# A streaming encoder step: half of w_out loaded per tile, and its SBUF given to gather slots and to a copy of the rows that the dots read

## The chip, the cores and the metric

The kernel runs on one core of one Trainium2 chip. The metric is the device time of one execution in microseconds (us). The engines are called by the profile's names: PE (TensorE), PEld (its weight loads), DVE (VectorE), ACT (ScalarE), POOL (GpSimd) and SP (SyncE).

## The reference

One layer over a prompt of 1024 rows and a sample of 32 rows, all in float32, D = 1024. The mixer (mLSTM and sliding-window attention, then w_out of 1024x1024) is followed by PEER, a mixture of 16384 single-row experts:

```
x = x + concat(mLSTM heads, attention heads) @ w_out
h = rmsnorm(x)
q = (h @ w_q)                         # 8 heads, 256 wide
idx = the 16 best of 128 x 128 experts for each row and head
a = gelu(sum over d of peer_u[idx] * h)       # 16 dots of 1024 for each row and head
x = x + sum over heads and k of (softmax weight * a) * peer_v[idx]
y = rmsnorm(x)
```

So each of the 1056 rows reads 8 x 16 rows of peer_u and as many of peer_v, 4 KB each.

## The kernel before, in words

**Tiles and groups.** Work is done in 9 tiles: 8 of 128 prompt rows and the sample's 32 (tile 8, SAMPLE). For PEER a tile is cut into blocks of 32 rows (SUB). 32 rows x 4 heads fill the 128 partitions, so a block has two groups of 4 heads, and there are 66 groups. In a group, k runs over the 16 chosen experts. For every (group, k) POOL issues one gather of peer_u (L582) and one of peer_v (L593): an indirect DMA of 128 rows of 4 KB, 512 KB, whose row numbers it reads from the SBUF tile `idx`. POOL alternates: U of group g + 1, then V of group g.

**Slots.** The tile `ring` holds NU = 6 U slots and NV = 7 V slots of 4 KB a partition. POOL waits on `u_free` before it writes into a U slot that is still used, and on `v_free` for a V slot, in one program order.

**DVE, ACT, PE for each slot t = 16 g + k.** DVE multiplies the U slot by `h2p` and sums up into `dots` (L1261, "the dot"; the accumulator is read by an instruction of its own). `h2p` is a PSUM tile that holds the block's 32 rows four times, once for each head. PE writes it in `spread_rows` (L1603) with 16 instructions, once every two groups, from the tile `ch`. Between dots DVE does a piece of `topk` for group g + 3 (11 of 16 slots), and at a group's turn `weigh` (L1210 to L1216), which makes the weights `wk` out of gelu (ACT, L821) and softmax. PE multiplies the V slot by `wk` into `acc` (L1657). In the same order of slots all engines do steps of the next tile's mixer, query projection and scores. The tables PE_AT, ACT_AT and DVE_AT and the function slot_of say at which slot. `attn_out` (L1504, L1505) is the last product of attention, `cat_transpose` and `h2_transpose` are L1513, `out_proj` is L1531, `residual` L1131, the query product L1549.

**Where h2p turns.** `spread_rows(q)` is called at k = 15 of an even group, and PE waits there for `dots_done`, since the dots still read `h2p`. DVE waits for `h2p_set` ahead of the next group's first dot. When g is odd DVE does `weigh(g)` and the first stage of `topk(g + 3)` before that wait ("ahead").

**Weights and SP.** One SBUF tile, `weights`, holds w_in in the start phase, then w_out (32 KB a partition, `wout_s`) and w_q (64 KB). w_out is loaded once, and used by tiles 1 to 8; tile 0 has its own copy in the ring. SP issues all plain DMAs in program order. In tile m these are `load_p(m)` (projection rows from a DRAM scratch), `store_y(m - 2)` and `load_x(m)`. Between tiles 3 and 4 `project_again` projects the rows of tiles 4 to 8 anew ("reprojection", L1365), with w_in streamed in pieces.

Of the kernel before, what the change touches and what calls it, by code (L numbers as in the profile page):

```python
# [48 lines left out]
SUB = 32  # L49
NU = 6  # L50
NV = 7
GROUPS = 2 * (SEQ // SUB + 1)
# [123 lines left out]
def program(nc, x_prompt, x_sample, cache_k, cache_v, st_c, st_n, st_m, norm_mix_w, w_in, if_bias, mnorm_w, sinks,  # L176
# [15 lines left out]
    with ExitStack() as ctx:  # L192
# [3 lines left out]
        def sem(name):  # L196
            return ctx.enter_context(nc.semaphore(name))
# [3 lines left out]
        win_s = [weights[:, DC * c0:DC * (c0 + w)].rearrange("p (k c) -> p k c", k=DC) for c0, w in PC]  # L201
        wout_s = weights[:, 0:DC * D].rearrange("p (k c) -> p k c", k=DC)
        wq_s = weights[:, DC * D:].rearrange("p (k c) -> p k c", k=DC)
        ring = sb("ring", [P, NU + NV, D])
        pj = sb("pj", [P, PJ])
# [12 lines left out]
        t8 = reg[:, 0:1024].rearrange("p (k t) -> p k t", k=DC)  # L218
        qrow = reg[:, 1024:1536]
        pT = pj[:, 0:2048].rearrange("p (h b t) -> p h b t", h=QH, b=2)  # L220
        qT = pj[:, 0:2048].rearrange("p (c t) -> p c t", c=QC)
# [69 lines left out]
        po = [sc[:, 4 * b:4 * b + 4, :].rearrange("p c k -> p (c k)") for b in range(4)]  # L291
        po += [part[:, :]] + [ring[:, NU + 4, 0:512]] + [a[:, h * 512:h * 512 + 512] for a in (ring[:, NU + 5, :], ring[:, NU + 6, :]) for h in range(2)]
        first = [pj[:, 0:512], pj[:, 512:1024], vx[:, :, 0:MD], pj[:, 1024:1536], pj[:, 1536:2048], pj[:, 2048:PJ]]
# [20 lines left out]
        proj_out = [sem(f"proj_out{b}") for b in range(10)]  # L314
        wout_in, wq_in = sem("wout_in"), sem("wq_in")
        keysT_ready, keysT_copied = sem("keysT_ready"), sem("keysT_copied")
        state_in, stateT_ready, state_set = sem("state_in"), sem("stateT_ready"), sem("state_set")
# [15 lines left out]
        wpiece_in, po_again_out = [sem(f"wpiece_in{i}") for i in range(3)], [sem("po_again_out0"), sem("po_again_out1")]  # L333
        topk_done, h2p_set = sem("topk_done"), sem("h2p_set")
        u_in = [sem(f"u_in{i}") for i in range(NU)]
# [22 lines left out]
        def _(sp):  # L358
# [79 lines left out]
            def load_wout():  # L438
                sp.dma_start(wout_s, w_out[0].rearrange("(k p) c -> p k c", p=P)).then_inc(wout_in, 16)

            def project_again():

                load_x1_again(FIRST)
                sp.wait_ge(query_ready, 4 * FIRST)
# [78 lines left out]
            for b in range(10):  # L523
                sp.wait_ge(proj_out[b], stored(b, len(UNITS)))
            for m in range(2, TILES):
                if m == FIRST:
# [13 lines left out]
                if m != FIRST:  # L540
                    load_p(m)
                store_y(m - 2)
                load_x(m)
# [12 lines left out]
        def _(pool):  # L556
# [16 lines left out]
            def gather_u(g, k):  # L573

                n = TOPK * g + k
                if k == 0:
                    pool.wait_ge(topk_done, g + 1)
                if n >= NU:
                    pool.wait_ge(u_free, n - NU + 1)
                elif n >= NU - 2:  # L580
                    pool.wait_ge(query_ready, 3)
                pool.indirect_dma_start(ring[:, n % NU, :], None, u_d,  # L582
                                        bass.IndirectOffsetOnAxis(ap=idx[:, g % 4, k:k + 1], axis=0)).then_inc(u_in[n % NU], 16)

            def gather_v(g, k):

                n = TOPK * g + k
                if n >= NV:
                    pool.wait_ge(v_free, n - NV + 1)
                elif n >= NV - 3:  # L590
                    for b in {NV - 3: (5,), NV - 2: (6, 7), NV - 1: (8, 9)}[n]:
                        pool.wait_ge(proj_out[b], stored(b, len(UNITS)))
                pool.indirect_dma_start(ring[:, NU + n % NV, :], None, v_d,  # L593
                                        bass.IndirectOffsetOnAxis(ap=idx[:, g % 4, k:k + 1], axis=0)).then_inc(v_in[n % NV], 16)
# [11 lines left out]
        def _(act):  # L606
# [211 lines left out]
            def gelu(g):  # L818
# [3 lines left out]
                act.drain().then_inc(gelu_ready, 1)  # L822

            def gather_parts(q):

                s = q % 4
                other = slice((s + 2) % 4 * SUB, (s + 2) % 4 * SUB + SUB)
                act.wait_ge(v_free, 2 * TOPK * (q + 1))
                if q == 0:
                    for b in (4,):  # L830
                        act.wait_ge(proj_out[b], stored(b, len(UNITS)))
                S.copy(part[other, :], acc[other, 512:])
                act.drain().then_inc(part_ready, 1)
# [21 lines left out]
            for s, i, r in ACT_AT:  # L855
                if r >= EARLY_END:
                    mix(s, i, 0)
                    if s == "query_copy" and i == 1:
                        keep_first()
            keep_scores(0)  # L860

            steps = by_slot(ACT_AT)
            for g in range(-1, GROUPS):
                for k in range(TOPK):
# [9 lines left out]
                    if k == TOPK - 1 and g + 1 < GROUPS:  # L874
                        gelu(g + 1)
                    for s, i, m in steps.get(t, ()):
                        mix(s, i, m)
# [25 lines left out]
        def _(dve):  # L903
# [347 lines left out]
            for g in range(-1, GROUPS - 1):  # L1251
                for k in range(TOPK):
# [5 lines left out]
                    if k == 0 and g % 2:  # L1258
                        dve.wait_ge(h2p_set, (g + 1) // 2 + 1)
                    dve.wait_ge(u_in[n % NU], 16 * (n // NU + 1))  # L1260
                    V.scalar_tensor_tensor(ring[:, n % NU, :], ring[:, n % NU, :], 1.0, h2p[:, :], ALU.mult, ALU.mult,  # L1261
                                           accum_out=dots[:, (g + 1) % 2, k:k + 1]).then_inc(u_free, 1)
# [35 lines left out]
        def _(pe):  # L1298
# [120 lines left out]
            def mix(s, i, m):  # L1419
# [100 lines left out]
                elif s == "out_proj":  # L1520
                    half, k0 = i // 4, i % 4 * 2
                    if i == 0:
# [4 lines left out]
                    if m == 0 and i % 4 == 0:  # L1527
                        pe.wait_ge(wout_first_in[half], 16)
                    for k in (k0, k0 + 1):
                        w = wout_first[half][:, k, :] if m == 0 else wout_s[:, k, half * 512:half * 512 + 512]  # L1530
                        last = T.matmul(mx[0:n, 2 + half, :], t8[:, k, 0:n], w, start=k == 0, stop=k == DC - 1)  # L1531
# [61 lines left out]
            def spread_rows(q):  # L1593
# [3 lines left out]
                if q > 0:  # L1597
                    pe.wait_ge(dots_done, 2 * q)
                pe.wait_ge(h2_ready, m + 1)
# [39 lines left out]
            for g in range(-1, GROUPS):  # L1639
                for k in range(TOPK):  # L1640
# [3 lines left out]
                    if k == 2 and g > 0 and g % 2 == 0:  # L1644
                        gather_parts(g // 2 - 1)
                    if k == TOPK - 1 and g % 2 == 0 and g + 2 < GROUPS:
                        spread_rows(g // 2 + 1)
                    if g >= 0 and t > 0:
# [4 lines left out]
                        for n in (0, 1) if t == 1 else (t,):  # L1653
                            pe.wait_ge(v_in[n % NV], 16 * (n // NV + 1))
                            for half in range(2):
                                cols, j = slice(half * 512, half * 512 + 512), (g // 2 + 2 * half) % 4 * SUB
                                last = T.matmul(acc[j:j + SUB, cols], wk[:, g % 2, n % TOPK, :], ring[:, NU + n % NV, cols],  # L1657
                                                start=g % 2 == 0 and n % TOPK == 0, stop=g % 2 == 1 and k == TOPK - 1)
# [59 lines left out]
```

## Time and profile before

| | |
|---|---|
| timed runs, median of 3 | 3127.24 us (3126.11 to 3127.49) |
| span of the profiled execution | 3386.3 us |
| mean granted clock of PE | 0.811 |
| gathers (L582 and L593) | 2112, 1107.43 MB |
| all DMA traffic | 1197.02 MB, 353 GB/s over the span |

The profiled execution is one of its own. The profile gives its span alone, from the first to the last instruction, and no time around it: 3386.3 us, 259 us more than the median of the timed runs. Durations of instructions come from the profiled one.

### The profile page before, as it was taken

The page shows a single profiled execution, that of the slowest core. Times are in us where ns is not written, and L with a number is a line of the kernel's source. Part 1 is how long each engine was busy: PE and PEld are TensorE (multiplying, and loading weights), DVE is VectorE, ACT ScalarE, POOL GpSimd, SP SyncE. Part 2 cuts the span into 40 slices and gives each one's busy share as a digit, 9 for nine tenths or more (in the row PEclk, how much of TensorE's full clock was granted, in tenths as well). Part 3 has the DMA queues.
Part 4 walks back from the last instruction along what each step waited for, and adds up shares of the span by engine and source line. Part 5 has one row for each costly group of instructions (what it writes and reads, how often), then busy time and mean ns, then how long its engine had stood idle before and what let it go on. Part 6 is the DMA issues. An engine that isn't in the chain of part 4 may idle for free.

```text
span 3386.3 us, 33673 instructions
## 1 busy us (share of the span) xinstructions
PE 2600.2 (77%) x10989; PEld 1007.2 (30%) x10989; DVE 2120.6 (63%) x5282; ACT 556.3 (16%) x1093; POOL 1995.2 (59%) x2128
## 2 busy tenths in 40 slices
PE   8996886678678899987876876678676776686666
PEld 4562351225222533223432331124212331121101
DVE  1256657766676666657667757676667666676653
ACT  2211111211121131122012111111111011111001
POOL 0026556666666566665656666666666666666665
PEclk9997897789677899997987887788667886677667
DMA  6479999999999999999999999999999999999998
GB/s 230 146 275 371 336 338 374 362 371 343 378 351 365 342 400 407 409 382 353 362 329 346 380 354 381 367 364 345 384 360 360 370 365 376 358 368 370 371 363 332
DMA packets 348919, 1197.02 MB, mean 353 GB/s; under 512 B 37760, under 2 KB 54408, under 8 KB 346952
## 3 DMA queue, kind: packets, MB, share of 16 engines
q0 software_dynamic: 304128, 1107.43, 86.7%
q1 hardware_dynamic: 44616, 87.45, 7.0%
q8 instruction: 86, 1.41, 0.2%
q14 instruction: 89, 0.73, 0.1%
HBM read 1180.69 MB, written 14.15 MB: 353 GB/s over the span
## 4 chain that ended last, share of the span: by engine, by line
PE 33%; DVE 16%; issue 13%; POOL 12%; DMA 9%; another core or an unknown queue 8%; DVEq 6%; ACT 1%; ACTq 0%; SPq 0%; POOLq 0%
PE acc L1657 11%; PE mx L1549 7%; DVE ring L1261 7%; POOL ring L593 6%; POOL ring L582 6%; DMA ring<-in_peer_v_dram,idx 5%; DVEq L1148 4%; DMA ring<-in_peer_u_dram,idx 4%; PE mx L1365 3%; PE mx L1531 2%; PE acc L1341 2%; PE mx L1560 2%; PE acc L1328 1%; PE h2p L1603 1%
## 5 line engine op out<-in xcount | busy, mean ns | idle before, releaser
L1657 PE MATMUL acc<-ring,wk 128*32 128x512 f32 x4224 | 1362.6, 742 | 525.6 <-DMA ring<-in_peer_v_dram,idx 289.4
L1261 DVE SCALAR_TENSOR_TENSOR ring<-ring,h2p 128x1024 f32<-128x1024 f32 x1056 | 1273.8, 1215 | 565.4 <-DMA ring<-in_peer_u_dram,idx 315.8
L593 POOL DMA_INDIRECT ring<-in_peer_v_dram,idx x1056 | 997.1, 944 | 707.7 <-issue 269.7
L582 POOL DMA_INDIRECT ring<-in_peer_u_dram,idx x1056 | 996.3, 943 | 667.1 <-issue 292.9
L1657 PEld LDWEIGHTS acc<-ring,wk 128*32 128x32 f32 x4224 | 217.8, 122 | 1406.6 <-issue 670.8
L1549 PE MATMUL mx<-reg,weights 128*128 128x128 f32 x1792 | 256.7, 297 | 40.9 <-issue 38.6
L1549 PEld LDWEIGHTS mx<-reg,weights 128*128 128x128 f32 x1792 | 230.8, 206 | 145.7 <-issue 145.7
L1531 PE MATMUL mx<-weights,reg 128*128 128x512 f32 (+1 forms) x256 | 133.0, 643 | 3.5 <-issue 3.5
L1365 PE MATMUL mx<-weights 128*128 128x512 f32 (+1 forms) x288 | 126.9, 585 | 0.0
L821 ACT ACTIVATE gl<-dots 128x16 f32<-128x16 f32 x66 | 14.2, 216 | 637.5 <-issue 346.1
L1603 PE MATMUL h2p<-ch,ident 32*32 32x512 f32 x528 | 86.7, 708 | 36.6 <-issue 18.9
L1560 PE MATMUL mx<-kT,pj 128*32 128x128 f32 x1040 | 69.4, 313 | 32.9 <-issue 25.3
L781 ACT COPY pj<-mx 128x512 f32<-128x512 f32 x32 | 18.7, 585 | 432.0 <-remote 182.7
L1261 DVE DVE_READ_ACCUMULATOR ring<-ring,h2p 128x1 f32 x1056 | 86.9, 82 | 0.0
L821 ACT ACT_TABLE_LOAD x66 | 84.7, 1283 | 6.5 <-issue 1.1
L815 ACT ACT_TABLE_LOAD x61 | 78.3, 1283 | 19.1 <-issue 11.3
L1365 PEld LDWEIGHTS mx<-weights 128*128 128x128 f32 x288 | 53.4, 195 | 75.8 <-issue 74.3
L1531 PEld LDWEIGHTS mx<-weights,reg 128*128 128x128 f32 (+1 forms) x256 | 44.1, 189 | 96.4 <-issue 96.4
L1560 PEld LDWEIGHTS mx<-kT,pj 128*32 128x32 f32 x1040 | 50.1, 123 | 64.6 <-issue 54.8
L1224 DVE TENSOR_TENSOR xt<-xt,acc 32x1024 f32<-32x1024 f32 x33 | 40.1, 1216 | 45.0 <-PE acc L1612 32.2
L1087 DVE TENSOR_REDUCE s<-mx 128x4 f32<-128x1024 f32 (+1 forms) x18 | 21.0, 1174 | 58.9 <-remote 46.6
L1365 PE MATMUL mx<-weights,reg 128*128 128x512 f32 (+1 forms) x96 | 47.4, 642 | 12.4 <-DMA weights<-in_w_in_dram 6.6
(310 smaller groups left out, 2400.3 us busy)
## 6 DMA issues: line engine op xcount, KB each, us to landing
ring<-in_peer_u_dram,idx POOLq DMA_INDIRECT x1056
ring<-in_peer_v_dram,idx POOLq DMA_INDIRECT x1056
weights<-in_peer_w_q_dram SPq DMA_DIRECT2D x7, 2048.0 KB
weights<-in_w_in_dram SPq DMA_DIRECT2D x5, 2048.0 KB, 18.2
weights<-in_w_in_dram SPq DMA_DIRECT2D x10, 1024.0 KB
ring<-in_peer_w_q_dram SPq DMA_DIRECT2D x8, 1024.0 KB, 5.6
xt<-in_x_prompt_dram SPq DMA_DIRECT2D x8, 512.0 KB
ring<-in_w_out_dram SPq DMA_DIRECT2D x2, 2048.0 KB, 14.2
```

Source lines behind the costliest of these rows:

```text
L582: pool.indirect_dma_start(ring[:, n % NU, :], None, u_d, bass.IndirectOffsetOnAxis(ap=idx[:, g % 4, k:k + 1], axis=0)).then_inc(u_in[n % N ...
L593: pool.indirect_dma_start(ring[:, NU + n % NV, :], None, v_d, bass.IndirectOffsetOnAxis(ap=idx[:, g % 4, k:k + 1], axis=0)).then_inc(v_in[ ...
L815: S.activation(ew[:, :], top[:, g % 3, :], ACT.Exp, bias=ntop[:, g % 3:g % 3 + 1], accum_out=ez[:, 0:1])
L821: S.activation(gl[:, :], dots[:, g % 2, :], ACT.Gelu)
L1148: dve.drain()
L1261: V.scalar_tensor_tensor(ring[:, n % NU, :], ring[:, n % NU, :], 1.0, h2p[:, :], ALU.mult, ALU.mult, accum_out=dots[:, (g + 1) % 2, k:k + ...
L1365: last = T.matmul(bank, hT1_again[i][:, 4 * half + k, :], wpiece[(2 * p + half) % 3][:, k, 0:w], start=half + k == 0, stop=half == 1 and k ...
L1531: last = T.matmul(mx[0:n, 2 + half, :], t8[:, k, 0:n], w, start=k == 0, stop=k == DC - 1)
L1549: last = T.matmul(mx[:, i // 4, i % 4 * P:i % 4 * P + n], w, t8[:, k, 0:n], start=k == 0, stop=k == DC - 1)
L1560: last = T.matmul(mx[q:q + SUB, i, col:col + NK], qT[:, c, i * SUB:(i + 1) * SUB], kT[:, c % 2, :], start=True, stop=True)
L1603: last = T.matmul(h2p[j * SUB:(j + 1) * SUB, cols], ident[r, r], ch[m % 2][r, cols], start=True, stop=True)
L1657: last = T.matmul(acc[j:j + SUB, cols], wk[:, g % 2, n % TOPK, :], ring[:, NU + n % NV, cols], start=g % 2 == 0 and n % TOPK == 0, stop=g ...
```

## The change

Of w_out only the first 4 of 8 row blocks (WK = 4) stay in `weights`. The other four, 512 KB each, are loaded again in each tile 1 to 8 by `pass_wout(m)` on SP: three into parts of `pj` and `reg` once attention is through (`attn_ready`), the last into `ch[m % 2]` once its transposes are done (`rows_transposed`). `out_proj` takes the products of both halves with blocks 0 to 6 first and with block 7 last. The 16 KB a partition that come free hold a seventh U slot, an eighth and a ninth V slot and `h2s`, an SBUF copy of `h2p` which ACT makes in `keep_rows`. The dot reads `h2s` in place of `h2p`. PE fills `h2p` at k = 4 of the even group, waiting only for the copy before; ACT copies it behind the gelu of the last group that reads the old rows. `project_again` gets a wait for `mixed_ready`.

```diff
-NU = 6
-NV = 7
+RU, RV = 6, 7
+NU = 7
+NV = 9
+WK = 4
...
-        wout_s = weights[:, 0:DC * D].rearrange("p (k c) -> p k c", k=DC)
+        wout_s = weights[:, 0:WK * D].rearrange("p (k c) -> p k c", k=WK)
...
+        spare = [weights[:, (WK + i) * D:(WK + i + 1) * D] for i in range(NU - RU + NV - RV)]
+        h2s = weights[:, (WK + 3) * D:(WK + 4) * D]
+        u_slot = [ring[:, b, :] for b in range(RU)] + spare[:NU - RU]
+        v_slot = [ring[:, RU + b, :] for b in range(RV)] + spare[NU - RU:]
...
+        wout_pass = [pj[:, 0:D], pj[:, D:2 * D], reg[:, D:2 * D]]
...
+            def pass_wout(m):
+                sp.wait_ge(attn_ready, m + 1)
+                for j in range(3):
+                    k = WK + j
+                    sp.dma_start(wout_pass[j], w_out[0, k * P:(k + 1) * P, :]).then_inc(wout_pass_in, 16)
+                sp.wait_ge(rows_transposed, 2 * m + 1)
+                sp.dma_start(ch[m % 2][:, :], w_out[0, (DC - 1) * P:DC * P, :]).then_inc(wout_last_in, 16)
...
             def project_again():
+                sp.wait_ge(mixed_ready, FIRST)
                 load_x1_again(FIRST)
...
             for m in range(2, TILES):
...
+                pass_wout(m)
                 store_y(m - 2)
                 load_x(m)
...
+            def keep_rows(q):
+                act.wait_ge(h2p_set, q + 1)
+                if q > 0:
+                    act.wait_ge(dots_done, 2 * q)
+                S.copy(h2s, h2p[:, :])
+                act.drain().then_inc(h2s_ready, 1)
...
                     if k == TOPK - 1 and g + 1 < GROUPS:
                         gelu(g + 1)
+                        if g >= 0 and g % 2 == 0 and g + 2 < GROUPS:
+                            keep_rows(g // 2 + 1)
...
-                        dve.wait_ge(h2p_set, (g + 1) // 2 + 1)
+                        dve.wait_ge(h2s_ready, (g + 1) // 2 + 1)
                     dve.wait_ge(u_in[n % NU], 16 * (n // NU + 1))
-                    V.scalar_tensor_tensor(ring[:, n % NU, :], ring[:, n % NU, :], 1.0, h2p[:, :], ALU.mult, ALU.mult,
+                    V.scalar_tensor_tensor(u_slot[n % NU], u_slot[n % NU], 1.0, h2s, ALU.mult, ALU.mult,
...
-                    half, k0 = i // 4, i % 4 * 2
+                    pairs = [(i // 4, i % 4 * 2 + a) for a in range(2)]
+                    if m > 0:
+                        pairs = [divmod(2 * i + a, DC - 1) for a in range(2)] if i < DC - 1 else [(0, DC - 1), (1, DC - 1)]
...
+                    if m > 0 and i == WK // 2:
+                        pe.wait_ge(wout_pass_in, 16 * 3 * m)
+                    if m > 0 and i == DC - 1:
+                        pe.wait_ge(wout_last_in, 16 * m)
...
                 if q > 0:
-                    pe.wait_ge(dots_done, 2 * q)
+                    pe.wait_ge(h2s_ready, q)
...
-                    if k == TOPK - 1 and g % 2 == 0 and g + 2 < GROUPS:
+                    if k == 4 and g >= 0 and g % 2 == 0 and g + 2 < GROUPS:
                         spread_rows(g // 2 + 1)
```

## Rows read from the trace of the kernel before

**Rows 1.** The page's first part: busy time, share of the span, instructions.
```profile
PE 2600.2 (77%) x10989; PEld 1007.2 (30%) x10989; DVE 2120.6 (63%) x5282; ACT 556.3 (16%) x1093; POOL 1995.2 (59%) x2128
```

**Rows 2.** The page's costliest groups: busy, mean ns, idle before and its releaser.
```profile
L1657 PE MATMUL acc<-ring,wk 128*32 128x512 f32 x4224 | 1362.6, 742 | 525.6 <-DMA ring<-in_peer_v_dram,idx 289.4
L1261 DVE SCALAR_TENSOR_TENSOR ring<-ring,h2p 128x1024 f32<-128x1024 f32 x1056 | 1273.8, 1215 | 565.4 <-DMA ring<-in_peer_u_dram,idx 315.8
L593 POOL DMA_INDIRECT ring<-in_peer_v_dram,idx x1056 | 997.1, 944 | 707.7 <-issue 269.7
L582 POOL DMA_INDIRECT ring<-in_peer_u_dram,idx x1056 | 996.3, 943 | 667.1 <-issue 292.9
```

**Rows 3.** The list of waits: us in total, times, longest.
```profile
POOL ring L582 <- DVEq L1204: 198.1, 6, 189.3
...
DVE ring L1261 <- remote: 89.0, 14, 9.7
...
DVE ring L1261 <- PE h2p L1603: 63.4, 14, 15.2
```

**Rows 4.** Timeline of POOL in the start: two long waits.
```profile
209.67 0.94 POOL L582 DMA_INDIRECT ring<-in_peer_u_dram,idx  x1 [9.13 <-DVE ring L1261]
...
259.67 0.94 POOL L593 DMA_INDIRECT ring<-in_peer_v_dram,idx  x1 [19.19 <-DMA proj_scratch<-ring]
```

**Rows 5.** Timeline of POOL, then of DVE, in a quiet stretch.
```profile
3163.36 0.94 POOL L582 DMA_INDIRECT ring<-in_peer_u_dram,idx  x1 [0.31 <-issue]
3164.61 0.94 POOL L593 DMA_INDIRECT ring<-in_peer_v_dram,idx  x1 [0.30 <-issue]
3165.85 0.94 POOL L582 DMA_INDIRECT ring<-in_peer_u_dram,idx  x1 [0.31 <-issue]
...
3164.78 1.22 DVE L1261 SCALAR_TENSOR_TENSOR ring<-ring,h2p 128x1024 f32<-128x1024 f32 x1 [1.32 <-DMA ring<-in_peer_u_dram,idx]
...
3167.35 1.22 DVE L1261 SCALAR_TENSOR_TENSOR ring<-ring,h2p 128x1024 f32<-128x1024 f32 x1 [1.34 <-DMA ring<-in_peer_u_dram,idx]
```

**Rows 6.** Windows: busy of PE, PEld, DVE, ACT, POOL; clock, DMA share, GB/s.
```profile
1300.00:1350.00 50.00, 47.10 (x154) 15.57 (x153) 31.75 (x75) 9.45 (x15) 32.54 (x35) 0.98 1.03 409
2400.00:2450.00 50.00, 33.91 (x105) 7.36 (x106) 30.83 (x76) 8.70 (x11) 33.55 (x36) 0.64 1.02 399
```

**Rows 7.** Timeline: gathers, and DVE instructions that began within half a microsecond.
```profile
259.23 1.22 DVE L1261 SCALAR_TENSOR_TENSOR ring<-ring,h2p 128x1024 f32<-128x1024 f32 x1 [3.29 <-DMA ring<-in_peer_u_dram,idx]
...
289.35 0.43 DVE L1193 TENSOR_TENSOR cand<-cand,i2f 128x256 f32<-128x256 f32 x1
289.44 1.15 POOL L593 DMA_INDIRECT ring<-in_peer_v_dram,idx  x1 [0.31 <-issue]
...
1018.36 0.69 DVE L1216 TENSOR_TENSOR wk<-rept,coef 128x512 f32<-128x512 f32 x1
1018.49 1.38 POOL L593 DMA_INDIRECT ring<-in_peer_v_dram,idx  x1 [0.30 <-PE acc L1657]
...
2477.14 0.93 POOL L582 DMA_INDIRECT ring<-in_peer_u_dram,idx  x1 [0.31 <-DVE ring L1261]
2477.28 0.69 DVE L1216 TENSOR_TENSOR wk<-rept,coef 128x512 f32<-128x512 f32 x1
```

**Rows 8.** Groups by form: busy, mean ns, idle before.
```profile
L1216 DVE TENSOR_TENSOR wk<-rept,coef 128x512 f32<-128x512 f32 x66 | 45.7, 693 | 6.3 <-issue 0.8 <-remote 0.5
...
L1035 DVE SCALAR_TENSOR_TENSOR pj<-pj,reg 128x512 f32<-128x512 f32 x8 | 5.5, 685 | 0.7 <-ACTq L721 0.7
...
L781 ACT COPY pj<-mx 128x512 f32<-128x512 f32 x32 | 18.7, 585 | 432.0 <-remote 182.7 <-PE mx L1549 171.2 <-issue 78.1
```

**Rows 9.** DMA issues with time to landing; timeline of PE in tile 4.
```profile
weights<-in_w_in_dram SPq DMA_DIRECT2D x1, 1056.0 KB, 17.3
...
1593.54 0.39 PE L1504 MATMUL mx<-vprev,pj 128*128 128x64 f32 x2
...
1614.44 1.12 PE L1531 MATMUL mx<-weights,reg 128*128 128x512 f32 x2
```

## What I predict, and how the numbers come about

> **What bounds the kernel now.** I read the busy line first: no engine is full, PE is busiest with 77% and it idles in between; POOL has 59%, DVE 63% [rows 1]. Shares say little here, because the same four workers take turns on every pair of gathers (one row set of peer_u for a dot on DVE, one of peer_v for a product on PE). So I read the groups of the page for POOL. Its 2112 gathers are busy 997.1 + 996.3 = 1993 us and have 707.7 + 667.1 = 1375 us of idle time in front of them [rows 2]. The timeline of a quiet stretch shows that two gathers issued without any wait start 1.245 us apart, 0.94 busy and 0.30 to 0.31 between [rows 5]. So 2111 x 0.31 = 654 us of that idle time is the cost of issuing, 189 us is the wait for the first indices [rows 3], and 1375 - 654 - 189 = about 532 us is waiting for a free slot. Two of these waits, 28 us together, belong to the start: a V slot that the projection still used, and the first U slots [rows 4]. That leaves about 504 us. POOL's chain is thus 190 + 1993 + 654 + 532 = 3369 us, and with the tail it is the span of 3386: **the kernel is set by POOL's issue, at 2.49 us a pair, plus 504 us of waiting for slots.**
>
> The second bound lies just under it. In the same stretch, where DVE waits for nothing but data, the dots start every 2.55 to 2.57 us while POOL issues every 2.49 [rows 5]: transfers land at 1.05 MB / 2.56 = 410 GB/s, the rate that the windows with the DMA engines at 1.03 also show (409) [rows 6]. A window of quieter work has 399 GB/s at 1.02. So POOL cannot win more than it loses to the DMA engines, 0.06 us a pair or about 65 us in all.
>
> **The change, part by part.**
>
> *Three more slots (U 6 to 7, V 7 to 9).* They act on the 504 us alone. A V slot stays taken while PE does the tile's own work, a U slot while DVE stands at the turn of a row block. Two V slots are 5 us of issue more before POOL stops, one U slot 2.5 us. In the reprojection (the window from 1300 to 1350 stands for it: PE busy 47.1 of 50 us and DMA at 1.03) they can do nothing, since PE and DMA are full [rows 6]; I leave 50 us of waits there and 50 us for stalls longer than the slots. Of 504 some 400 go, less the 65 that DMA does not allow: **gain 335 us**, bounds 150 (slots fill again wherever PE is behind) and 440.
>
> *Spread in PSUM at index 4, copy h2s.* Before, spread_rows waits for the last dot and DVE for spread_rows: 63.4 + 89.0 = 152 us in 28 waits of DVE [rows 3]. Now the spread is done 11 slots earlier, and behind the last dot stands gelu and then an ACT copy of 128x1024. The copy of 128x512 takes 585 ns from PSUM [rows 8], so twice that, 1.2 us. DVE meanwhile has weigh (its product alone is 693 ns [rows 8]) and stage 0 of topk, so the copy costs nothing there; without that cover it would be 33 x 1.2 = 40 us. ACT has 16% of busy time [rows 1], 39 us more hide. The 152 us are waits of DVE, and they reach POOL only as U slots that come free late: they are within the 504 and I don't count them again. What is late next is gelu and the product's coefficients, unchanged.
>
> *The dot reads two SBUF tensors.* This is the disputed cost, in two halves. The duration: a two-SBUF SCALAR_TENSOR_TENSOR of 128x512 takes 685 ns, no more than those with a PSUM input, so I keep 1.215 us [rows 8, 2]. The other half is POOL. The trace has 2112 gathers, nearly all of 0.94 us, and the longer ones have a two-SBUF DVE instruction over their start. A gather that began 0.13 us after a 0.69 us product of rept and coef took 1.38; one that began 0.09 us after a 0.43 us product of cand and i2f took 1.15; one that began 0.14 us before such a product took 0.93 [rows 7]. In each, the gather runs on about 0.12 us before the DVE instruction's end: the stretch is (DVE duration - 0.12 - distance of the starts). Today's dot, whose second input is in PSUM, stretches none: a gather that began 0.44 us after a dot took 0.94 [rows 4, 7], and the mean of all is 943 to 944 ns [rows 2]. For a dot of 1.215 us the stretch is up to 1.04 and 0.52 on average. If gathers start at random against dots, 1056 x 1.04 / 3180 = 35% of them are caught: 0.18 us each, **380 us in all**. That is the upper bound. The lower is near 0.06 us a pair, 65 us: where dots come every 2.56 us and POOL could issue every 2.49, POOL's starts drift forward against the dots by 0.07 us a pair and meet a dot at its trailing end, where a stretch costs just the drift, and then stay there [rows 5]. Topk and the mixing steps break that rhythm often. I take the middle, **200 us**.
>
> The Trainium skill, page "SBUF — State Buffer", section "Who interferes with whom", says that a DVE instruction with at most one SBUF input doesn't contend with GpSimd, and that one with two contends with a GpSimd instruction that reads SBUF. By that rule, the trace agrees for gathers that start under such an instruction (1.38 and 1.15 against 0.94) and speaks against this edit; the sum above would be the same.
>
> *w_out in parts.* Four row blocks of 512 KB for each of 8 tiles, less 2 MB of the one load: 14.7 MB, 36 us at 410 GB/s. POOL, slowed by the stretches, leaves the DMA engines room, so most of it hides; without that room it is 36. They stand in SP's queue behind attn_ready and ahead of store_y and load_x. A load of 1056 KB landed 17.3 us after issue, 61 GB/s [rows 9], so three parts take 20 to 25 us. In tile 4 PE's attention ends at 1593.9 and the third step of out_proj, now the first to need them (the first two use the four resident rows), starts at 1614.4 [rows 9]: up to 5 us late, and load_x behind them can hold DVE's residual, with the dots queued behind it. Other tiles have 25 us or more. I take **40 us** for traffic and lateness together, bounds 0 and 100. project_again now waits for mixed_ready of tile 3, and behind it on SP only the wait for query_ready, which comes later anyway: nothing. The order of out_proj's 16 products changes, not their number: nothing.
>
> **Sum.** -335 + 200 + 40 = -95 us on the profiled 3386 (-2.8%). The timed median is 3127, 259 us less for the same work. Either issue and transfers are quicker without the profiler (then the terms stand), or there are fewer waits to take away (then 504 - 259 = 245 are left, the gain is about 180, and the sum +60). Between them, leaning to the first: -57 us, **3070 us**.
>
> **Rivals.**
> - *The stretch costs little and the slots give all they can* (gathers lock to the dots' ends). -335 + 65 + 20 = -250, 3127 - 190 = 2940 after the same discount. For it: the steady rhythm. Against: 11 of 16 dots have topk pieces between them.
> - *The stretch at random, and too few waits to pay for it.* POOL then needs 2.49 + 0.36 = 2.85 us a pair. With a gain of 220, between my 335 and the lower bound, 380 + 40 - 220 = +200; where PE or DMA is the bound anyway (a third, by the 504 us and the windows like the reprojection) stretches hide: +125, about 3250. It decides as soon as the mean stretch of a gather passes (gain - 40) / 2112: 0.14 us in the profile's budget, 0.07 to 0.10 if the timed run has half of the waits.
> - *DMA is the bound of the timed run already*: slots bring nothing, the stretch hides, and 14.7 MB are added: 3127 + 5 to 40, say 3145.
> - *The dot slows down.* Here is no row of a two-SBUF product with an accumulator. At twice 1.215 us DVE is busy 2120.6 + 1273.8 = 3394 us [rows 1, 2] and becomes the bound: about 3450. For it nothing but that gap in the rows; the 685 ns row speaks against. The Trainium skill, "Vector Engine (DVE) Microarchitecture Reference", section "Points that are easy to get wrong", says that this instruction with two sources in SBUF that aren't bf16 runs at half throughput. By that rule, the trace disagrees where there is no accumulator; with one no run here shows it.
>
> **How the numbers follow.** Forecast 0.37, locked gathers 0.20, random stretch 0.27, DMA-bound 0.10, slow dot 0.06. A difference under 0.2% can't be told from none here. The forecast and the locked case are faster (0.57, of which 0.02 falls within 0.2%); DMA-bound gives 0.05 to no change; the rest is slower: 0.55, 0.07, 0.38. The range takes the forecast with its bounds and reaches toward both neighbours: 2960 to 3260.
>
> **What would show it.** L593 and L582: mean above 943 ns (1.04 at 200 us of stretch, 1.13 at 380), with their idle time down from 1375 to about 950. L1261: still 1215 ns, and its waits for PE's spread gone. The row of keep_rows near 1.1 us x33. Out_proj's first product with a streamed row: a wait in tile 4 at most. The forecast is wrong if the idle time of the gathers does not fall, if the stretch is at its upper bound, or if L1261 changes its duration.

## The result, and the profile after

The changed kernel takes 3251.66 us (median of 4 runs, 3249.96 to 3255.37); the kernel before took 3126.68 us beside it (4 runs, 3124.94 to 3127.49). The ratio is 1.0401 (1.0387 to 1.0416): 125 us slower, where 3070 us and a gain of 57 us were forecast. The measured time lies at the far end of the stated range (2960 to 3260), and it is the time that the second rival gave.

The page of the changed kernel, its busy line, traffic, the chain that ended last, the groups that answer to [rows 1, 2], and two issue lines (count, kilobytes each where given, us to landing):

```profile
PE 2571.2 (79%) x10989; PEld 958.5 (30%) x10989; DVE 2142.5 (66%) x5282; ACT 589.5 (18%) x1126; POOL 2304.2 (71%) x2128
...
DMA packets 353017, 1211.72 MB, mean 373 GB/s; under 512 B 38272, under 2 KB 54920, under 8 KB 351048
...
POOL 33%; PE 30%; DMA 19%; issue 12%; DVE 4%; DVEq 1%; ACT 1%; SPq 0%; ACTq 0%; POOLq 0%
...
L1294 DVE SCALAR_TENSOR_TENSOR ring<-ring,weights 128x1024 f32<-128x1024 f32 x906 | 1106.0, 1223 | 578.5 <-DMA ring<-in_peer_u_dram,idx 549.3
...
L604 POOL DMA_INDIRECT ring<-in_peer_u_dram,idx x906 | 977.3, 1079 | 523.7 <-issue 263.5
L615 POOL DMA_INDIRECT ring<-in_peer_v_dram,idx x822 | 902.5, 1098 | 270.6 <-issue 216.2
...
L615 POOL DMA_INDIRECT weights<-in_peer_v_dram,idx x234 | 259.9, 1111 | 71.9 <-issue 62.2
...
L604 POOL DMA_INDIRECT weights<-in_peer_u_dram,idx x150 | 162.7, 1084 | 60.4 <-issue 43.3
...
L1576 PE MATMUL mx<-weights,reg 128*128 128x512 f32 (+1 forms) x128 | 71.3, 673 | 0.1
...
ring<-in_peer_u_dram,idx POOLq DMA_INDIRECT x906, 7.5
...
pj<-in_w_out_dram SPq DMA_DIRECT2D x16, 512.0 KB, 8.1
```

L604, L615 and L1294 are the U gather, the V gather and the dot; an operand in the memory that w_out gave up is named `weights`. POOL's 2112 gathers are now busy 2302 us (mean 1.09) where they had 1993, and idle for 523.7 + 60.4 + 270.6 + 71.9 = 927 us where they had 1375 [rows 2]. With 654 us of issue gaps and 190 before the first indices, 83 us of slot waits are left. POOL's chain is 190 + 2302 + 654 + 83 = 3229, and with a tail of 19 it is the span of 3248.2. The execution behind this span took 3249.96 us: **span and time of one execution lie 2 us apart, not 259.** The 259 us of the profile ahead of the prediction must be a difference between executions.

The timeline of POOL and of DVE in a quiet stretch of the changed kernel answers to [rows 5, 7]:

```profile
3061.30 1.82 POOL L615 DMA_INDIRECT ring<-in_peer_v_dram,idx  x1 [0.30 <-PE acc L1702]
3063.43 0.93 POOL L604 DMA_INDIRECT ring<-in_peer_u_dram,idx  x1 [0.30 <-issue]
3064.66 0.99 POOL L615 DMA_INDIRECT ring<-in_peer_v_dram,idx  x1 [0.30 <-PE acc L1702]
3065.96 1.05 POOL L604 DMA_INDIRECT ring<-in_peer_u_dram,idx  x1 [0.30 <-issue]
...
3061.08 1.23 DVE L1294 SCALAR_TENSOR_TENSOR ring<-ring,weights 128x1024 f32<-128x1024 f32 x1 [1.61 <-DMA ring<-in_peer_u_dram,idx]
3062.23 0.08 DVE L1294 DVE_READ_ACCUMULATOR ring<-ring,weights 128x1 f32 x1
...
3063.62 1.22 DVE L1294 SCALAR_TENSOR_TENSOR weights<-weights 128x1024 f32<-128x1024 f32 x1 [0.72 <-DMA weights<-in_peer_u_dram,idx]
...
3065.78 0.42 DVE L1226 TENSOR_TENSOR cand<-cand,i2f 128x256 f32<-128x256 f32 x1
```

The first gather begins 0.22 us after a dot and takes 1.82 us: the rule of the prediction gives 1.23 - 0.12 - 0.22 = 0.89 over 0.94. The third begins 1.04 us after a dot and takes 0.99, by the rule 0.94 + 0.06. The fourth meets no dot but a product of two SBUF tiles that the kernel before has too: 0.42 - 0.12 - 0.18 over 0.94 is 1.06, and it takes 1.05. The dot itself is no longer for it (1.22 to 1.23 us). POOL waits 0.30 us before each, which is the bare issue gap, so every stretch moves all that follows.

Counted over the whole trace of the changed kernel, 680 gathers begin between 0.07 and 1.05 us after a dot's start, and 679 of them last within 0.05 us of what the rule gives (with 0.943 for a gather without a stretch). The 824 gathers that begin up to 1.1 us after a dot's start carry 291 us of stretch. In before_2, a trace of the kernel before from a chip of the same speed, the 814 such gathers carry none.

### The profile page after: what moved, and what is told of

The parts are those of the page before. It is cut to its first block, busy times and chain, and to the rows that moved or that the text cites. A ratio compares the mean times of both kernels' runs of the same rounds, so it can differ in the third digit from the quotient of the medians.

```text
span 3248.2 us, 33803 instructions
## 1 busy us (share of the span) xinstructions
PE 2571.2 (79%) x10989; PEld 958.5 (30%) x10989; DVE 2142.5 (66%) x5282; ACT 589.5 (18%) x1126; POOL 2304.2 (71%) x2128
## 4 chain that ended last, share of the span: by engine, by line
POOL 33%; PE 30%; DMA 19%; issue 12%; DVE 4%; DVEq 1%; ACT 1%; SPq 0%; ACTq 0%; POOLq 0%
POOL ring L604 14%; POOL ring L615 14%; PE acc L1702 10%; DMA ring<-in_peer_v_dram,idx 10%; PE mx L1594 6%; DMA ring<-in_peer_u_dram,idx 4%; POOL weights L615 3%; DMA weights<-in_peer_v_dram,idx 3%; POOL weights L604 2%; PE mx L1576 2%; PE acc L1374 2%; PE mx L1398 1%; PE acc L1361 1%; PE h2p L1648 1%; DVE ring L1294 1%
## 5 line engine op out<-in xcount | busy, mean ns | idle before, releaser
L1294 DVE SCALAR_TENSOR_TENSOR ring<-ring,weights 128x1024 f32<-128x1024 f32 x906 | 1106.0, 1223 | 578.5 <-DMA ring<-in_peer_u_dram,idx 549.3
L1702 PE MATMUL acc<-ring,wk 128*32 128x512 f32 x3288 | 1088.4, 757 | 499.2 <-DMA ring<-in_peer_v_dram,idx 423.4
L604 POOL DMA_INDIRECT ring<-in_peer_u_dram,idx x906 | 977.3, 1079 | 523.7 <-issue 263.5
L615 POOL DMA_INDIRECT ring<-in_peer_v_dram,idx x822 | 902.5, 1098 | 270.6 <-issue 216.2
L1702 PEld LDWEIGHTS acc<-ring,wk 128*32 128x32 f32 x3288 | 151.4, 121 | 1221.2 <-DMA ring<-in_peer_v_dram,idx 876.1
L1702 PE MATMUL acc<-weights,wk 128*32 128x512 f32 x936 | 311.1, 757 | 122.9 <-DMA weights<-in_peer_v_dram,idx 107.5
L615 POOL DMA_INDIRECT weights<-in_peer_v_dram,idx x234 | 259.9, 1111 | 71.9 <-issue 62.2
L1294 DVE SCALAR_TENSOR_TENSOR weights<-weights 128x1024 f32<-128x1024 f32 x150 | 183.6, 1224 | 92.5 <-DMA weights<-in_peer_u_dram,idx 90.0
L604 POOL DMA_INDIRECT weights<-in_peer_u_dram,idx x150 | 162.7, 1084 | 60.4 <-issue 43.3
L1294 DVE DVE_READ_ACCUMULATOR ring<-ring,weights 128x1 f32 x906 | 74.6, 82 | 0.0
L1576 PE MATMUL mx<-weights,reg 128*128 128x512 f32 (+1 forms) x128 | 71.3, 673 | 0.1
L1257 DVE TENSOR_TENSOR xt<-xt,acc 32x1024 f32<-32x1024 f32 x33 | 40.1, 1216 | 24.0 <-PE acc L1657 23.2
```

The source lines that it names most:

```text
L604: pool.indirect_dma_start(u_slot[n % NU], None, u_d, bass.IndirectOffsetOnAxis(ap=idx[:, g % 4, k:k + 1], axis=0)).then_inc(u_in[n % NU], 16)
L615: pool.indirect_dma_start(v_slot[n % NV], None, v_d, bass.IndirectOffsetOnAxis(ap=idx[:, g % 4, k:k + 1], axis=0)).then_inc(v_in[n % NV], 16)
L1257: V.tensor_tensor(xt[m % 2][r, :], xt[m % 2][r, :], acc[r, :], ALU.add)
L1294: V.scalar_tensor_tensor(u_slot[n % NU], u_slot[n % NU], 1.0, h2s, ALU.mult, ALU.mult, accum_out=dots[:, (g + 1) % 2, k:k + 1]).then_inc(u ...
```

## The experiments

The theory: the dot's second SBUF input stretches the gathers and makes POOL the bound, and the slots bring little, because the timed runs lack the waits that they were to remove. Rivals: the cost comes from the streamed w_out, from the early spread with its copy, or from the longer queue of gathers. The dot's operand and the streamed w_out were run alone, the slots on top of the streamed w_out, whose memory they need; the early spread was never run without the copy. The runs fell on four chips (A to D here). On A and B the kernel before takes 3125.6 (9 runs) and 3126.9 us (9), as in the comparison; on C and D it takes 3414.7 (21) and 3393.7 us (8). The recorded texts call C and D slow chips. Each chip was used in one session only, so what belongs to the chip and what to the session isn't told apart. A ratio is always against the kernel before on the same chip.

All results first; slot waits are worked out from each page as above (idle time of the gathers - 654 - 190). Gathers and slot waits are in us.

| run | chip | ratio to before (interval) | span profiled | gathers busy | slot waits |
|---|---|---|---|---|---|
| before_2 | A | one run, 3128.7 us | 3127.0 | 1996 | 268 |
| wout_only_2 | B | 1.0117 (1.0101 to 1.0132) | 3163.9 | 1995 | 306 |
| slots_only_2 | A | 1.0099 (1.0084 to 1.0115) | 3156.8 | 1999 | 293 |
| fewer_slots | A | 1.0206 (1.0192 to 1.0220) | 3181.0 | 1998 | 322 |
| dot_sbuf_2 | A | 1.0441 (1.0417 to 1.0465) | 3270.5 | 2328 | 79 |
| copy_only_2 | B | 1.0473 (1.0452 to 1.0495) | 3274.7 | 2327 | 85 |
| before_again | C | one run, 3421.8 us | 3420.1 | 1993 | 565 |
| wout_only | C | 0.9997 (0.9977 to 1.0017) | 3409.8 | 1995 | 553 |
| slots_only | C | 1.0110 (1.0087 to 1.0134) | 3454.4 | 1995 | 598 |
| dot_sbuf | C | 1.0044 (1.0026 to 1.0062) | 3425.5 | 2350 | 214 |
| after_again | D | 1.0091 (1.0063 to 1.0120) | 3421.8 | 2326 | 232 |
| copy_only | D | 1.0034 (1.0014 to 1.0054) | 3394.9 | 2336 | 197 |

**The dot with two SBUF inputs alone** (dot_sbuf on C, dot_sbuf_2 on A). The kernel before, whose dot reads other SBUF data in place of `h2p`: a row of a constant mask, 128 wide and read 8 times. It leaves out the right dots, so the output is not the reference's; sizes, waits and traffic are the same.

```diff
-V.scalar_tensor_tensor(ring[:, n % NU, :], ring[:, n % NU, :], 1.0, h2p[:, :], ALU.mult, ...
+V.scalar_tensor_tensor(ring[:, n % NU, :], ring[:, n % NU, :], 1.0, triu[:, :].unsqueeze(1).broadcast_to([P, DC, P]), ALU.mult, ...
```

> The kernel before with one edit: the dot's second input is an SBUF constant (triu, repeated 8 times) in place of h2p in PSUM. It leaves the right dots out, so y is not the reference's; indices, gathers, waits and all durations' shapes are those of before. Theory (a dot with two SBUF inputs holds up the start of a gather): POOL's busy time rises by 280 to 380 us, of which the 270 us of slot waits hide a part: 3230 to 3330 us. Rival (the loss of the changed kernel comes from w_out's traffic and its place in SP's queue): 3127. Rival (the dot itself is slower with two SBUF inputs): L1261's mean above 1.3 us; the theory says 1.22.

> The kernel before with the dot's second input an SBUF constant; it leaves the right dots out. Theory A: on a slow chip +0.4% again, since a POOL that issues later leaves PE its instructions (issue idle 195 in place of 300) and the 360 us of stretch fit into 570 us of waits; on a chip that takes 3127 there are 270 us of waits, so +120 to +200 us: 3250 to 3330. Theory B (the loss of the changed kernel has another cause than the dot's operand): +0.4% there too.

On A this one edit costs 4.4%, 143 us, more than the whole change: inside the 120 to 200 us of the theory, and against the rivals. The groups of its page:

```profile
L1261 DVE SCALAR_TENSOR_TENSOR ring<-ring,triu 128x1024 f32<-128x1024 f32 x1056 | 1287.8, 1223 | 719.9 <-DMA ring<-in_peer_u_dram,idx 671.5
...
L582 POOL DMA_INDIRECT ring<-in_peer_u_dram,idx x1056 | 1148.1, 1087 | 565.9 <-issue 310.6
L593 POOL DMA_INDIRECT ring<-in_peer_v_dram,idx x1056 | 1180.3, 1118 | 357.0 <-issue 261.2
```

Its gathers are 332 us longer than before_2's, and its slot waits fell by 189 us with not one slot more: 332 - 189 = 143. POOL comes late, so the slots are free when it comes. On C the same stretch (357 us longer) is met by 351 us fewer waits, and the edit costs 0.4%: dot_sbuf's 3230 to 3330 us, expected before C was known to be slower, were missed.

**The kernel before, again** (before_again on C, before_2 on A).

> The kernel before, unchanged, for a trace beside its timed runs. The profiled execution on which the prediction rested had a span of 3386 us, its timed runs 3127. In the changed kernel span and time are 2 us apart (3248.2 and 3249.96). Expected: span near 3125; gathers 943 to 944 ns and starts 1.24 us apart as before, so that waits for slots are 3125 - 190 - 1995 - 654 - 16 = 270 us in place of 532. If the longer execution had slower issue instead, the gap between gathers is below 0.30 us here and the waits stay near 500.

> The kernel before, for a trace. So far its traces are from chips on which it takes 3386 to 3420 us; in them PE is idle 294 to 307 us for nothing that the profile shows (issue), in the changed kernel's trace from the chip of the comparison 6 us. Expected where this chip takes 3127: issue idle of PE under 40 us and slot waits of POOL near 270. Expected where it takes about 3400: both as before, 300 and 530 to 570.

before_again missed its expected 3125 by 297 us: chip C is slower. By its likeness the profile ahead of the prediction was taken on such a chip too; which one it was isn't on record. before_2 came as expected (268 us of slot waits, under 40 us of pauses on PE). The list of waits of PE in before_again, then of before_2 (us in total, times, longest):

```profile
PE acc L1657 <- DMA ring<-in_peer_v_dram,idx: 285.3, 208, 6.4
PE acc L1657 <- issue: 138.0, 122, 6.0
...
PE mx L1549 <- issue: 43.0, 36, 3.9
```

```profile
PE acc L1657 <- DMA ring<-in_peer_v_dram,idx: 449.5, 420, 5.8
...
PE mx L1549 <- issue: 3.5, 1, 3.5
```

Gathers, dots and ACT's instructions last the same on both, and so does POOL's gap of 0.30 us. PE does not: it is busy 2607 us on C and 2519 on A, at a mean granted clock of 0.814 and 0.839. And on C PE stands for 300 us (24 rows of this list together) in short pauses "issue", in which it waits for nothing that the profile shows; on A for 4 us. In the profile ahead of the prediction they make 291 us. With PE late, the V slots come free late: the gathers of V are idle 713.5 us on C and 421.5 on A, those of U 695.6 and 690.0, and the slot waits are 565 us against 268. On A PE waits for data instead. The bound is seen in before_2: the slices of GB/s, the traffic, the chain that ended last, and the whole stretch behind the start as a window (its last three numbers are clock, DMA share and GB/s).

```profile
GB/s 246 117 245 389 409 360 401 409 392 408 408 408 403 394 400 408 408 404 366 377 390 380 410 408 409 406 408 406 404 391 410 406 409 388 403 370 409 410 409 336
DMA packets 348919, 1197.02 MB, mean 383 GB/s; under 512 B 37760, under 2 KB 54408, under 8 KB 346952
...
DMA 35%; PE 34%; DVE 12%; POOL 9%; issue 6%; DVEq 4%; ACT 1%; SPq 0%; ACTq 0%; POOLq 0%
...
234.50:3127.00 2892.50, 2297.95 (x10008) 824.72 (x10006) 2064.09 (x5087) 505.23 (x988) 1976.22 (x2091) 0.83 1.01 397
```

Behind the start it moves 397 GB/s, 97% of the 410 that none of its slices passes, and DMA has the largest share of the chain, if only just ahead of PE. The next two experiments bear it out: **the kernel before is bound by its transfers on such a chip.**

**w_out in parts alone** (wout_only on C, wout_only_2 on B): the changed kernel with NU = 6, NV = 7, the dot reading `h2p`, the old spread and no copy.

```diff
-NU = 7
-NV = 9
+NU = 6
+NV = 7
...
-                        dve.wait_ge(h2s_ready, (g + 1) // 2 + 1)
+                        dve.wait_ge(h2p_set, (g + 1) // 2 + 1)
...
-                    V.scalar_tensor_tensor(u_slot[n % NU], u_slot[n % NU], 1.0, h2s, ALU.mult, ALU.mult,
+                    V.scalar_tensor_tensor(u_slot[n % NU], u_slot[n % NU], 1.0, h2p[:, :], ALU.mult, ALU.mult,
...
-                    pe.wait_ge(h2s_ready, q)
+                    pe.wait_ge(dots_done, 2 * q)
...
-                    if k == 4 and g >= 0 and g % 2 == 0 and g + 2 < GROUPS:
+                    if k == TOPK - 1 and g % 2 == 0 and g + 2 < GROUPS:
```

> Only the streamed half of w_out: 6 U and 7 V slots, dot and spread as before. Theory: POOL has 270 us of waits that are not issue, so traffic of 14.7 MB (36 us at 410 GB/s) shows in part: +15 to +40, 3140 to 3165. Rival (traffic or late rows are the loss of the change): 3250. A wait of out_proj for its streamed rows would show in tile 4 first, under 5 us.

> The kernel before with half of w_out streamed per tile and nothing else: 6 U and 7 V slots, the dot reads h2p in PSUM, spread late. On a chip like that of before_2 (3125.6), where slots_only_2 took 3156.6. If the DMA engines bound the kernel and extra slots only lengthen the queue in front of them, the 14.7 MB cost the same as in slots_only_2: 14.7 MB at 383 GB/s is 38 us at most, so 3150 to 3163 (ratio 1.008 to 1.012). Rival: the longer queue costs by itself (a direct DMA such as load_x lands later behind 9 V slots), and the traffic hides in the waits: 3127 to 3140, ratio under 1.005. Third: the slots bring something and the traffic costs more than it carries: over 3165. On a chip where PE idles for 300 us without a cause in the profile, as in wout_only, the ratio should be 0.998 to 1.002 again.

On B it costs 1.2%, 37 us, close to the first expectation (3150 to 3163; it takes 3164). The traffic line of its page has the same rate as that of before_2, 383 GB/s, and 14.7 MB more; 14.7 / 0.383 = 38 us:

```profile
DMA packets 353016, 1211.71 MB, mean 383 GB/s; under 512 B 38272, under 2 KB 54920, under 8 KB 351048
...
ring<-in_peer_u_dram,idx POOLq DMA_INDIRECT x1056, 12.4
```

On C it costs nothing that can be measured, and the 3140 to 3165 us of wout_only were missed with the chip. There the rate is 355 GB/s over the span, so the transfers seem to have room; the page's busy share of the DMA engines is no measure of it, with 0.97 at 366 GB/s in the profile ahead of the prediction.

**The slots** (slots_only on C, slots_only_2 on A: as wout_only, but 7 U and 9 V slots; fewer_slots on A: 6 U and 5 V).

> The changed kernel without the copy: the dot reads h2p in PSUM, spread_rows at index 15 behind dots_done as before; U 7, V 9 and the streamed half of w_out stay. Theory (the stretch alone is the loss): gathers back at 943 ns, slot waits from 270 down to about 100, the 14.7 MB cost up to 36 us: 3127 - 170 + 30 = about 2990, between 2940 and 3060. Rival (traffic or late rows are the loss): 3200 or more. Rival (the early turn of the rows was what took the waits away, not the slots): about 3127 + 30.

> Slots and the streamed half of w_out, dot from PSUM, late spread: as slots_only. Theory A (PE starves for instructions when gathers stand deep in the DMA engines' queues, on some chips): on a slow chip slower than before by 1% again with PE's issue idle near 380; on a chip that takes 3127, 2940 to 3060, the slots' full worth. Theory B (more slots just don't help): not faster on either.

> As slots_only, but with 6 U slots and 5 V slots. Theory A: PE's issue idle falls below the 307 of 6 and 7 slots, and the time stays within 1% of before on a slow chip although two slots are gone; on a chip that takes 3127 each slot counts and it is 3250 or more. Theory B (waits for slots are the same loss everywhere): slower by 3% or more on both.

The slots' full worth, 2940 to 3060 us, came on neither chip: theory B of slots_only_2 holds. Of fewer_slots both theories miss, 3186 us where one wanted 3250 and the other 3% or more.

On A and B 6 and 7 slots, 7 and 9 slots, and 6 and 5 slots give 1.0117, 1.0099 and 1.0206 with the same traffic. Two V slots fewer cost 0.9%; three slots more bring 0.2%, about the size of the intervals. What they do change is the time from issue to landing. To the 12.4 us of wout_only_2 above belong, in the pages of slots_only_2 and fewer_slots:

```profile
ring<-in_peer_u_dram,idx POOLq DMA_INDIRECT x906, 15.4
```

```profile
ring<-in_peer_u_dram,idx POOLq DMA_INDIRECT x1056, 9.0
```

POOL fills each added slot, its transfer joins the queue (512 KB at 410 GB/s are 1.3 us, 3.8 for three), and the gathers land 3.0 us later. The rate is 383 GB/s with 13 slots and 384 with 16, and POOL's waits for slots go from 306 to 293 us: they are mostly the DMA bound seen from POOL, and three slots don't remove them. On C the three slots even cost 1.1% beside wout_only's 0.0%, and PE's pauses "issue" grow from 300 to 384 us. That deeper gather queues delay PE's own supply of instructions would fit; no run shows it, and fewer_slots, which would have tested it there, fell on A.

**The copy, the early spread and the SBUF dot, without new slots** (copy_only on D, copy_only_2 on B), and the changed kernel on D (after_again).

```diff
-NU = 7
-NV = 9
+NU = 6
+NV = 7
```

> The changed kernel with the old number of slots (6 and 7): the copy, the early spread and the streamed half of w_out stay. Theory (the stretch of the gathers is the cost, the slots' share is what lies between this and the changed kernel): POOL busy near 2300 us as in the changed kernel, slot waits between its 83 and the 222 of the dot that reads SBUF with the late spread; so 20 to 120 us above the changed kernel on the same chip. If the slots bring nothing once POOL is slower, equal to it.

> The changed kernel, unchanged. The chip of the first four experiments runs the kernel before in 3403 to 3426 us, where the chip of the comparison took 3125 to 3127, and the profile on which the prediction rested (span 3386) looks like the former. Both comparisons in one call show what the change does on whichever chip this is. If POOL's issue sets the changed kernel (190 + 2304 + 654 + 83 us), its time hardly depends on the chip: 3250 to 3290 here too, so faster by 4% where before takes 3414 and slower by 4% where it takes 3127. If transfers set it on such a chip, as the 3452 of the slots alone suggests, it is 3430 to 3480.

> The changed kernel with 6 U and 7 V slots in place of 7 and 9 (copy h2s, early spread and streamed w_out stay). On a chip like that of before_2, where the kernel after took 3251.7 and dot_sbuf_2 3268.6. POOL is the bound there: 190 of start + 2330 busy + 654 of issue gaps = 3174, and slot waits on top (83 in the kernel after with 7 and 9 slots, 89 in dot_sbuf_2 with 6 and 7). If the slots are what makes the kernel after 17 us shorter than dot_sbuf_2 in spite of its extra traffic, copy_only_2 is longer than after by some 20 to 40 us: 3270 to 3290, with slot waits of 100 to 130 us. If it is the early spread with its copy, copy_only_2 stays within 8 us of after: 3245 to 3260, slot waits of 75 to 95 us. Either way the mean gather stays at 1.09 to 1.11 us.

On B, copy_only_2 takes 1.0473, the changed kernel in the comparison 1.0401: once POOL is the bound the three slots bring some 22 us, in two sessions and with a wide spread (the five runs of copy_only_2 lie from 3265.7 to 3284.9). Its time was expected (3270 to 3290), its slot waits (100 to 130) were not: they are equal to those of the changed kernel, 85 and 83 us. The difference lies in the gathers, 2327 and 2302 us busy. These are its groups:

```profile
L604 POOL DMA_INDIRECT ring<-in_peer_u_dram,idx x1056 | 1148.4, 1087 | 569.8 <-issue 310.4
L615 POOL DMA_INDIRECT ring<-in_peer_v_dram,idx x1056 | 1178.1, 1116 | 359.0 <-issue 270.6
```

With more slots a gather meets a dot at another point, on average a better one: of copy_only_2 858 gathers begin up to 1.1 us after a dot's start and carry 315 us of stretch, of the changed kernel 824 with 291. Why is not settled. Against dot_sbuf_2, copy_only_2 adds the streamed w_out, the copy and the early spread, and costs 0.3% more. So most of the 37 us of traffic hides once the transfers are no longer the bound, unless the early spread gives back as much; no run parts the two. On D the changed kernel costs 0.9% and copy_only 0.3%: there the sign of the slots' effect is the other one, as on C. Both expectations for D are missed: after_again takes 3423 us and neither 3250 to 3290 nor 3430 to 3480, and copy_only is not 20 to 120 us above the changed kernel but 20 below it.

No version tried beats the kernel before; what the early spread would bring beside a dot that still reads PSUM was not tried.

## Why the prediction was wrong

**The waits that the slots were to remove (504 us, gain 335): this step failed.** The 504 us were read rightly, but in an execution with 291 us of such pauses on PE. On a chip as fast as that of the timed runs there are 268 us, 240 without the 28 of the start, close to the 245 that the prediction gave for "fewer waits to take away". And those are mostly no buffering stalls: they are the DMA bound. The prediction took 65 us off for it, from 410 GB/s against POOL's 2.49 us a pair. By slots_only_2 against wout_only_2 the gain is about 6 us. This could have been seen ahead: the 1197 MB are 353 GB/s over the profiled span, but 383 over the timed 3127 us. By an estimate from the rates shown (47.5 MB in the first 234.5 us, as in before_2, and the other 1164 MB at 410 GB/s), the changed kernel would take about 3075 us with no pause in its transfers at all, so the forecast of 3070 lay at the ceiling itself.

**The 259 us between profile and median: the choice between the two readings failed.** Gathers of 942 and 949 ns and gaps of 0.30 us stand in before_2 too, whose span of 3127.0 lies 2 us under its time. So issue is no quicker in the timed runs, nor is the ceiling of 410 GB/s another. The second reading, which gave +60, was right; with the measured stretch in place of 200 it gives -180 + 309 + 40 = +169, of which most of the 40 is hidden.

**The stretch (taken 200, bounds 65 to 380): the mechanism was right, the size was not.** It measured 2302 - 1993 = 309 us. The rule, DVE duration - 0.12 - distance, holds over the whole trace; by it the most is 1.22 - 0.12 = 1.10 us and not the prediction's 1.04, which would put the upper bound near 420. The locking to the dots' ends does happen (484 gathers begin 0.95 to 1.25 us after a dot's start, in before_2 218), but 824 of the 2112 gathers still begin over a dot, about as many as the 814 of before_2, where nothing holds them, and a gather loses 0.15 us on average; with the 0.07 to 0.10 that the second rival named as its point of decision, it decides. The Trainium skill, page "SBUF — State Buffer", section "Who interferes with whom", lets the two contend for an exclusive lock when DVE reads two SBUF inputs and the GpSimd instruction reads SBUF. The trace agrees for POOL, 943 to 1090 ns; the dot itself hardly pays, 1216 to 1223.

**What the sum became.** From before_2 to the changed kernel: gathers +306, slot waits 268 - 83 = -185, together +121, and the spans differ by 121.2. The waits look like the forecast gain, but dot_sbuf_2 loses 189 of them with no new slot: they went because POOL came late. Nor could the signs that the prediction named tell: the idle time of the gathers fell to 927 us, where it wanted 950, and their mean rose to 1.09 us, inside its 1.04 to 1.13. Against before_2 the idle time fell only from 1112.

**The dot's duration: right.** 1223 ns. The Trainium skill, "Vector Engine (DVE) Microarchitecture Reference", section "Points that are easy to get wrong", has this instruction with two SBUF sources that aren't bf16 at half throughput; with the accumulator too, the trace disagrees, and the fourth rival falls.

**w_out (taken 40, bounds 0 to 100): right in size, in another place.** Alone it costs 37 us, all traffic. No product waits for its rows (L1576 0.1 us idle, and 0.0 in the groups that read `pj` and `ch`, below), and 512 KB into `pj` land after 8.1 us, so the lateness in tile 4 did not come. In the changed kernel it seems mostly hidden, as the prediction said of a POOL slowed by stretches.

```profile
L1576 PE MATMUL mx<-pj,reg 128*128 128x512 f32 x56 | 28.8, 617 | 0.0
...
L1576 PE MATMUL mx<-ch,reg 128*128 128x512 f32 x28 | 13.9, 619 | 0.0
```

**The early spread and the copy: as forecast, but for one wait.** The 33 copies take 1.01 us each. DVE's waits for the spread are gone, 50.6 us in before_2, and two waits for the copy, 14.1 us, have come. Its worth is not told apart by a run; the dots now wait more for data, 549.3 + 90.0 us in the changed kernel against 483.5 in before_2.

**The rivals.** The second rival's time of 3250 was hit. Its mechanism, too few waits to pay for the stretch, is the one that the runs show, but that the number fits so well is luck: it took a stretch of 380 and a gain of 220 by the slots, and measured are 309 and some 6 to 22. What pays for the stretch are the 189 us of waits that go without any slot. The third, a DMA bound already in the kernel before, is what slots_only_2 shows (3156.6 against its 3145), but the stretch doesn't hide: it moves the bound to POOL.

## What to carry to other kernels

Ahead of counting waits in a profile, compare its span with the timed runs: when they differ by 8%, as here, the waits may belong to that execution alone, and the price of an edit should be worked out once with them and once without. Divide the traffic by the timed runs, too, and not only by the span. Waits for free buffers are worth buffers only if the transfers behind them are not at their own ceiling; if the landing time grows with the buffers and the rate stays, the queue is the bound. On a chain that POOL issues, hold every long DVE instruction to at most one SBUF input, even where its own duration doesn't change by it.

## What the runs showed of the hardware that was not expected

- Chips (each in one session) differ by 9% on one kernel: 3126 and 3127 us on two, 3394 and 3415 us on two others, with gathers, dots and ACT's instructions alike. Of the 293 us between before_2 and before_again PE is busy for 88 and idle for 205, and within the idle time the pauses without a visible cause grow from 4 us to 300. The same change costs 4.0% on one kind and 0.9% on the other, where more slot waits, 565 us in place of 268, are there to take up the stretch.
- An indirect gather is held at its start by a DVE instruction with two SBUF inputs until 0.12 us before that one's end: 1.82 us in place of 0.94 where it began 0.22 us after a dot, while DVE loses 7 ns of 1216.
- With half of w_out streamed, the rate over the whole span is 381 GB/s with 11 slots, 383 with 13 and 384 with 16; the landing time goes with the slots: 9.0, 12.4 and 15.4 us.
